# A fused decoder on one core: scores of paired heads, regrouped by contraction height and moved by one place

## The reference, cut to what matters

```python
# MLA: 16 heads; a query and a key are 64 latent columns and 32 rotary columns
q_full = concatenate([q[..., :64], q_rope], -1)
k_full = concatenate([kv[..., :64], broadcast(k_rope)], -1)
s = einsum('bqhd,bkhd->bhqk', q_full, k_full) * scale        # causal
o = softmax(s) @ v
y = (o * silu(gate)) @ w_out
# SWA: 16 query heads, 4 key heads, 64 columns, no rotary part, window of 128 keys,
# a slope on the distance, and a sink in the softmax's sum
```

## Time and profile before

| | |
|---|---|
| median of 3 runs | 2031.86 us (2031.55 to 2037.02) |
| the profiled execution, its own time | 2036.35 us |
| its span, first to last instruction | 2034.6 us |
| PE busy | 1831.3 us, 90% |
| DVE, ACT, POOL busy | 841.6, 777.7 and 596.3 us |
| mean granted TensorE clock | 0.937 of full speed |
| attention of the first MLA layer | about 89 to 272 us from the span's start |
| attention of the SWA layer | about 366 to 500 us |
| attention of the second MLA layer | about 995 to 1180 us |

### The profile page before, as it was taken

How to read it: one execution, slowest core, us unless ns; L and a number is a source line. 1 busy time by engine, 2 the same in 40 slices (tenths; PEclk the granted TensorE clock), 3 DMA queues, 4 the chain that set the end, 5 groups by cost and what they waited for, 6 DMA issues and landing times.

```text
span 2034.6 us, 23634 instructions
## 1 busy us (share of the span) xinstructions
PE 1831.3 (90%) x9152; PEld 1446.1 (71%) x9152; DVE 841.6 (41%) x1831; ACT 777.7 (38%) x1556; POOL 596.3 (29%) x291
## 2 busy tenths in 40 slices
PE   7898998999789999898899997978778999999978
PEld 6676676787558788576666677757647788788767
DVE  2556625585513444543565633666453111000141
ACT  4445533464233544513454623323344332212242
POOL 4222222321323322114321123222202544444422
PEclk9999998999889999998999997788889999999989
DMA  5211133388433222123221134122101333223311
GB/s 144 54 37 47 55 125 108 75 84 63 119 82 84 67 69 63 32 85 84 49 55 47 42 115 126 52 62 73 45 26 55 111 97 93 93 93 94 114 53 72
DMA packets 214794, 154.98 MB, mean 76 GB/s; under 512 B 54107, under 2 KB 197227, under 8 KB 214684
## 3 DMA queue, kind: packets, MB, share of 16 engines
q1 hardware_dynamic: 205072, 128.37, 22.5%
q10 hardware_dynamic: 9308, 24.83, 7.1%
q0 software_dynamic: 304, 0.28, 0.1%
HBM read 144.38 MB, written 8.91 MB: 75 GB/s over the span
## 4 chain that ended last, share of the span: by engine, by line
PE 63%; DVE 12%; ACT 4%; issue 2%; ACTq 1%; POOL 0%; POOLq 0%; DVEq 0%
PE banks L446 18%; PE banks L447 17%; PE banks L448 17%; PE banks L556 2%; DVE AB L1826 2%; PE banks L598 1%; PE banks L622 1%; PE banks L637 1%; PE banks L545 1%; PE banks L606 1%; DVE AB L1922 1%; DVE AB L1920 1%; DVE AB L1913 1%; DVE QKl L1649 1%; PE banks L761 1%
## 5 line engine op out<-in xcount | busy, mean ns | idle before, releaser
L2239 POOL TENSOR_TENSOR w_lo<-w_raw,w_hi 128x1024 fp32r<-128x1024 f32 (+3 forms) x255 | 583.9, 2295 | 1406.7 <-ACT w_hi L1076 1406.7
L446 PE MATMUL banks<-XTh,w_hi 128*128 128x512 f32 (+1 forms) x1088 | 438.3, 403 | 19.2 <-DVE XTl L1869 7.6
L447 PE MATMUL banks<-XTl,w_hi 128*128 128x512 f32 (+1 forms) x1088 | 431.2, 396 | 0.0
L448 PE MATMUL banks<-XTh,w_lo 128*128 128x512 f32 (+1 forms) x1088 | 430.0, 395 | 0.0
L1076 ACT ACTIVATE w_hi<-w_raw 128x1024 fp32r<-128x1024 f32 (+3 forms) x255 | 253.4, 1002 | 245.9 <-PE banks L448 174.1
L446 PEld LDWEIGHTS banks<-XTh,w_hi 128*128 128x128 f32 x1088 | 208.6, 192 | 71.8 <-issue 17.9
L448 PEld LDWEIGHTS banks<-XTh,w_lo 128*128 128x128 f32 x1088 | 208.1, 191 | 46.0 <-issue 1.1
L447 PEld LDWEIGHTS banks<-XTl,w_hi 128*128 128x128 f32 x1088 | 208.7, 192 | 45.1 <-issue 2.6
L446 PE MATMUL banks<-w_hi,OTh 128*128 128x512 f32 (+1 forms) x448 | 174.0, 388 | 16.4 <-POOL w_lo L2239 6.6
L447 PE MATMUL banks<-w_lo,OTh 128*128 128x512 f32 (+1 forms) x448 | 170.9, 382 | 0.0
L448 PE MATMUL banks<-w_hi,OTl 128*128 128x512 f32 (+1 forms) x448 | 170.8, 381 | 0.0
(11 more groups left out here) (199 smaller groups left out, 2693.0 us busy)
## 6 DMA issues: line engine op xcount, KB each, us to landing
w_raw<-in_w_gate_up_dram SPq DMA_DIRECT2D x44, 512.0 KB, 3.8
w_raw<-in_fox_w_in_dram SPq DMA_DIRECT2D x32, 512.0 KB, 4.0
w_raw<-in_mla_w_in_dram SPq DMA_DIRECT2D x26, 512.0 KB, 3.9
w_raw<-in_w_in_dram SPq DMA_DIRECT2D x24, 512.0 KB, 3.7
w_raw<-in_w_down_dram SPq DMA_DIRECT2D x22, 512.0 KB, 3.5
w_raw<-in_swa_w_in_dram SPq DMA_DIRECT2D x20, 512.0 KB, 3.8
w_raw<-in_mla_w_out_dram SPq DMA_DIRECT2D x16, 512.0 KB, 3.6
w_raw<-in_mla_w_kv_up_dram SPq DMA_DIRECT2D x32, 128.0 KB, 2.8
```

Of the source, the lines that this page charges most:

```text
L446: nc.tensor.matmul(o, ah, bh, start=first, stop=False, skip_group_check=True)
L447: nc.tensor.matmul(o, ah, bl, start=False, stop=False, skip_group_check=True)
L448: return nc.tensor.matmul(o, al, bh, start=False, stop=last, skip_group_check=True)
L2239: pool.tensor_tensor(view(w_lo, u, RING), view(w_raw, u, RAW), view(w_hi, u, RING).bitcast(F32), ALU.subtract).then_inc(lo_done, 1)
```

## The change

Three things are edited, all in the program of PE. In `scores`, the loop over the tiles of a chunk is split: first the latent matmuls of all its tiles, then the rotary ones of all its tiles. Since the second tile's matmuls now come while the first tile's sum in the same bank is still open, only the first tile of a chunk carries the `start` flag. Only MLA's chunk (2, 0) has both two tiles and a rotary part, so its order alone changes. In `step`, S1 and T10 change places.

```diff
@@ -588,17 +588,19 @@
+                    def at(t):
+                        return (slice(t * P, (t + 1) * P), slice((t + 1) * P - pr.keys[t], (t + 1) * P),
+                                slice(pr.s_col(t), pr.s_col(t) + pr.keys[t]))
+
                     for t in pr.s_chunks[ch]:
-                        ts = slice(t * P, (t + 1) * P)
-                        ks = slice((t + 1) * P - pr.keys[t], (t + 1) * P)
-                        cols = slice(pr.s_col(t), pr.s_col(t) + pr.keys[t])
+                        ts, ks, cols = at(t)
                         for n, (qp, kp) in enumerate(((QKh, QKh), (QKh, QKl), (QKl, QKh))):
                             for x in range(2):
                                 r = slice(HD * x, HD * x + HD)
                                 mm = nc.tensor.matmul(bank[2 * (c.sch % 2) + x][:, cols], qp[r, pr.q, ts], kp[r, pr.k, ks],
-                                                      start=n == 0, stop=n == 2 and not pr.rope, skip_group_check=True)
-                        if not pr.rope:
-                            continue
+                                                      start=n == 0 and t == pr.s_chunks[ch][0], stop=n == 2 and not pr.rope, skip_group_check=True)
+                    for t in pr.s_chunks[ch] if pr.rope else ():
+                        ts, ks, cols = at(t)
                         rq, rk, r0 = pr.rope
@@ -651,9 +653,9 @@
                     elif n == 4:
+                        turn(i, 1, 0)
+                    elif n == 5:
                         scores(i + 2, 1)
-                    elif n == 5:
-                        turn(i, 1, 0)
                     elif n == 6:
```

## The result

The changed kernel took 2020.14 us (median of 6 runs, 2019.53 to 2026.0), the kernel before 2035.06 beside it: ratio 0.9936 (95% interval 0.9918 to 0.9954). So it is faster by 0.5 to 0.6%, by these ratios 10 to 13 us, with intervals that go from 7 to 17. The forecast was 2026.0, 5.9 us of gain.

A forecast was written before the change was run, and what follows sets the result against it. TensorE was taken to bound the kernel (63% of the chain), though not in every iteration. MLA's 8.6 us gain less SWA's 2.7 gave 5.9, so 2026.0 from 2031.86; own range 2022 to 2031, with rivals 2019 to 2034.

The forecast's parts named there:

- rival A: MLA and SWA: T10 never waits, VectorE and ScalarE follow TensorE, the gain passes in full: 9.7 us less, 2022; chance 0.22.
- The height change: TensorE's matmuls: changing contraction height costs 0.10 us on leaving, plus 0.05 on the first pair of 128 columns.
- T12's wait: MLA iterations 0 to 5: 0.53 us lost waiting for the copy of T10; the swap ends it.
- T10's new waits: After the swap T10 waits for a copy: 0.21 us in MLA iterations 1, 3, 5; 0.29 in SWA iterations 1 to 5.
- VectorE's wait: TensorE's wait for VectorE behind MLA iterations 1 and 3: to grow from 2.90 us by 0.3, to about 3.2.
- rival C: SWA: T10's new wait makes TensorE's clock fall, 1.6 us each; six falls lose 3.5 net, 2035; chance 0.09.
- the regrouped chunk: MLA's chunk (2, 0), 8 times a layer: two leavings and two first pairs gone, 0.30 us of 2.40; ends 0.20 and 0.30.
- Iterations -2 and -1 have no transposes: 0.30 each.: MLA start: these two iterations gain only the regrouping, 0.30 us each, 0.60 a layer.
- Iteration 5: MLA iteration 5: gains 0.83 us less T10's wait of 0.21, so 0.62.
- SWA: 3.4 for 2.7: SWA: the swap splits chunks of one height; iterations 1 to 4 lose 0.59 us each, iteration 0 0.30, 2.7 in all.
- iteration 5's 0.66, called hidden: SWA iteration 5: its loss is hidden behind the table writes, TensorE's end wait of 6.57 us shrinking by 0.6; otherwise 0.6 more lost.

The follow-up runs named there:

- e4: Changed kernel with MLA's chunk (2, 0) computed pass by pass, six blocks of one height instead of two: 2035.11 us, ratio 1.0017 to the kernel before.
- e6: Kernel before, with only POOL held until VectorE has normalized, for the one weight unit that ScalarE splits between its exponentials: 2022.76 us, ratio 0.9958.
- e9: Changed kernel with four tiny VectorE memsets delaying the normalization in iteration -1 of both MLA layers: 2028.82 us, ratio 0.9978 to the kernel before.
- e1: Kernel before with only the regrouping of latent and rotary matmuls, S1 and T10 not swapped: 2022.73 us against 2030.81, ratio 0.9957.
- e3: Changed kernel with S1 and T10 swapped in the MLA layers alone, SWA keeping its old order: 2019.52 us, ratio 0.9944 to the kernel before.
- e10: Changed kernel, but swap only in even MLA iterations and POOL held until the normalization in MLA iterations -1, 1, 3: 2013.11 us, ratio 0.9902 to before.
- e7: Kernel before with eight more matmuls in the second tile of weights, meant to start everything behind later: 2036.16 us, ratio 1.0015.
- e2: Kernel before with only S1 and T10 swapped, the chunk (2, 0) in its old order: 2033.28 us, ratio 1.0007.

## Why the prediction was right, and where it wasn't

**Right in kind, too small in size.** The forecast gain was 5.9 us; the stages give 8.2, the ratios 10 to 13. The measured 2020.14 lies under the forecast's own range of 2022 to 2031, and within the wide one of 2019 to 2034 only by the end that rival A's mechanism gave it: that is luck. The mechanisms forecast are there. The height change costs, and two of four blocks are gone (e4 and the rows of S0). T12's wait was lost whole, T10's new waits are 0.24 in odd iterations of MLA and 0.31 in SWA (0.65 less iteration 0's 0.34; worked out were 0.21 and 0.29), VectorE's wait grew to 3.14, SWA lost 0.34 and 0.65 an iteration (0.30 and 0.59). The granted clock in SWA stayed at 1.00, so rival C's mechanism didn't happen. Rival A came near in time (2022) for the wrong reason: T10 does wait.

**Mis-sized: the regrouped chunk.** It gains 0.39 and not 0.30, since a narrow pair behind a wide one costs 0.05 less than behind one of its own width, at both heights. That makes at most 16 x 0.09 = 1.4 us. I had put the range's doubt on the other side, 0.20.

**The step that failed: "Iterations -2 and -1 have no transposes: 0.30 each."** They gain 2.34 a layer instead of 0.60. I costed VectorE's work by its old duration. The 1.33 that TensorE waits there before, and the 3.4 us of four instructions that take 1.28 elsewhere, stand in the trace of before, and I hadn't looked at either: I took the 2.90 behind iterations 1 and 3 as given by ScalarE's exponentials, when three quarters of it were POOL's subtraction. Of the excess 1.74 a layer, 1.56 is the collision (1.56 in e6, 1.6 in e9) and 0.18 the chunk.

**Iteration 5: 0.19 for 0.62.** I took the time of ScalarE's copy from iteration 3, 2.31 behind T00. In iteration 5 VectorE is later with the output of pair 4, and the copy begins 2.57 behind T00, 2.85 in after (second MLA layer). Then T02 itself waits. TensorE of after, second MLA layer:

```profile
1130.29 1.11 PE L624 MATMUL banks<-ident,AB 128*128 128x128 f32 x6 [0.47 <-ACT AB L1224]
```

In i = 6, where no scores come between, 0.24 is lost (e1 12.50, e3 12.74). It is lost to the swap in i = 5, not to that in i = 6: e10, which swaps in 6 and not in 5, takes 16.21 and 12.51, and e3 15.94 and 12.74, 28.72 and 28.68 for the two (first MLA layer). So the swap in iteration 5 only moves time from one to the other. Why i = 6 starts its copy later I haven't followed.

**SWA: 3.4 for 2.7.** Iterations 0 to 4 lose 2.9, since the new height changes and T10's wait are each a little dearer than worked out. Of iteration 5's 0.66, called hidden, 0.17 comes back in i = 6. That the table writes hide the rest isn't borne out: TensorE's wait there didn't shrink by 0.6 but grew from 6.57 to 7.75, and from the last T00 to the next MLA layer's first score kernels with the swap in SWA take 505.03 to 505.78 us and those without it 504.99 to 505.51 (e7 aside, 508.49 with one more fall of the clock).

**The clock, and what is open.** The mechanisms give 8.2 to 8.6 us and the ratios 10 to 13. The later ratio's interval (7.3 to 12.8 us) holds 8.2, the first one's (9.4 to 16.7) doesn't. In the profiled pair 2.45 us lie ahead of all edited code. Its time at the lower clock went from 258 us to 247, and 1.5 us of the difference has a place, at the first MLA layer's start. There the clock fell in 3 of 8 traced starts of kernels that have S0 in the old order (before, e2, e6, e7), in both of e4, and in none of 18 starts with the new one. e9 had the collision and no fall, so the wait alone doesn't bring it. Whether the order of S0 does is open; no run was made for it. Open too is why the ratio was 0.9936 once and 0.9950 later; their intervals overlap.

## What to carry to other kernels

Ahead of costing a reorder of one engine, look in the timeline for instructions of the same shape that take two to three times as long in one place as in another: such a collision was worth more here than the edit, and a shift of 0.4 us relative to the other engine ended it, one of half a microsecond brought it back. Where a chunk uses two contraction heights, do all of one and then all of the other, wide tile first. Check a new wait against the rows of its own iteration, not against a neighbour's, and where a stall goes away undeservedly, put the edge that guarantees it into the program (here POOL's hold, 8 to 10 us for one wait).

## What the hardware showed

VectorE and GpSimd exclude each other on some operations. Four SBUF-to-SBUF multiplications by a column of scalars, 128 to 512 wide, took 1.28 us, and 3.40 to 3.42 with one GpSimd subtraction of 128 x 1024 that started 0.4 to 0.8 us behind the first. A VectorE sum with both inputs in SBUF took 0.69, and 1.86 when it began 1.09 behind the start of such a subtraction: that ended at 149.47, the sum at 150.03. A VectorE sum from PSUM beside it kept its 0.69 (e6, L1676 and L1680; after, 1001.94). The subtraction itself took 2.57 and 2.58 in the second layer's start, before and after, and 2.38 to 2.40 in e9, though a multiplication was under way when it started there too; why they differ is open. The Trainium skill has the rule, in "SBUF — State Buffer", who interferes with whom: the pair of ports that both use is held exclusively for a whole instruction, by a VectorE operation in a two-port mode, or by one with two SBUF inputs against a GpSimd operation that reads SBUF, and whoever comes second is blocked fully. The trace agrees: the sum at 148.17 was through 0.56 after POOL was, and the last multiplication of before (1006.99) 0.28 after. Had I held it against the 3.41, it would have pointed at POOL for the wait at the start.

A change of the contraction height between 64 and 32 cost 0.145 us net in e4, and 0.195 where the narrow pair's saving of 0.05 isn't in it. In the regrouped chunk two changes were worth 0.39 together, in which that saving is counted twice: 0.145 for a change whose first pair is 128 wide.
